# A transformer stack on one Trainium2 core: masks added by VectorE, paired heads in the fourth attention, and output projections with tokens on partitions

## The chip, the core and the metric

The kernel is one program on one core of a Trainium2 chip. Its engines run side by side: TensorE (PE, with its weight loads shown as PEld), VectorE (DVE), ScalarE (ACT), GpSimd (POOL) and SyncE (SP), which here issues DMAs. They meet through semaphores. SBUF and PSUM have 128 partitions; PSUM has eight banks of 512 fp32 columns. The metric is the device time of one execution in microseconds, lower is better.

## The reference

All tensors are fp32. The input is 512 tokens of width 1024 (and 256 context tokens). The first block has two attention layers, the second an even layer (attention and a gated linear recurrence, HGRN), a convolutional feed-forward network (FFN), an odd layer (attention with a relative bias) and a second FFN:

```python
s_loc = jnp.where(valid, s_loc, NEG_INF)                       # attention A: window of 128, sinks, 256 context keys
p = jax.nn.softmax(jnp.concatenate([s_loc, s_ctx, sink], axis=-1), axis=-1)
s = (einsum(qn_b, kn_all) + einsum(qr_b, kr_all)) * scale      # attention B: latent keys, no mask
s = jnp.where(valid, s, -jnp.inf)                              # attention E: chunks of 64, two before, sinks
s = s + bias.reshape(Hkv, G, CHUNK, band)                      # attention O: bias = rel_table[:, clip(i - j)]
c = conv_b + sum(conv_w[j] * u_pad[:, j:j + S]); y = (gelu(c) * v) @ w_down
h = h + rms_norm(y, nw[1])                                     # behind each mixer and each FFN (nw[3])
y = rms_norm(h, nw[2])                                         # ahead of the next one
```

## The kernel before

**Layout.** Activations are kept with features on partitions: `XC[:, k, token]` for the eight groups k of 128 features. Every product is fp32 precision made of three fp32r matmuls: high by high, low by high, high by low (L365 to L367, 512 columns each). Operands are split once: ACT rounds to the high part (`HH`, `WH`) and DVE or POOL subtract to get the low part (`HL`, `WL`). Weights come in panels of 512 KB that SP loads into three slots (`raww`, L1380); ACT writes `WH` (L317) and POOL `WL` (L1481), also three slots each. `lin_bank` takes seven PSUM banks in turn; `claim` makes PE wait until a bank's last reader is done.

**The attentions.** A has 32 jobs (16 heads, four query tiles of 128 rows, and two context tiles, a pair of heads at a time), B 16 heads, E 8 and O 16, with four query tiles each. `finish_att` writes the order of steps down. At step t PE makes the scores of tile t in one of two pairs of banks (`att_scores`, L543), transposes the probabilities of tile t-2 (L615) and multiplies by V, 64 output rows of a head at a time (L651). DVE takes the row maximum (L553; with sinks L556, then L557 on one column), ACT the exponent and its sum (L568) into `PB`, and DVE or ACT copy the transposes out of PSUM into `PT` (L633, L635). Masks of A and E are a bf16 matmul of a mask by the identity into the scores' bank (`maskb`, `identb`). In O the bias is two more matmuls, `flip` by `o_bh` and `flip` by `o_bl`, whose two parts POOL makes per head from a strip `o_band` (L1452, L1454); each O head has its q parts stacked in the 128 rows of `o_q2` and its k parts doubled in `o_kh`, `o_kl` (L1316 to L1320 on ACT, L1329 and L1333 on DVE, 64 rows each). The reciprocals of a pair's sums are turned and spread over 64 rows each by matmuls of 64 output rows (L594: 16 per pair of four tiles, 8 per context pair).

**Out projections and norms.** `e_o`, `o_o` and the down projections give features on partitions: weights are stationary, 512 tokens move (`out_lin`, `ffn_pe`). Down is made in three parts, of 8, 7 and 7 groups of the 22, that DVE adds up. The norm behind each of them (stages s01, s03, s11, s13) needs a sum over partitions: ACT squares (L396), POOL adds (L379), PE sums with ones (L387), ACT takes the root (L406, L409), DVE the reciprocal (L507), and PE spreads it over partitions (L516). Then per k DVE scales (L2419) and adds (L2424), ACT makes `HH` (L467) and a square for the next norm (L471), DVE makes `HL` (L486), and PE starts the next product. L448 sums those squares, four k at a time.

**The end.** The last down part (stage s13) is turned back to tokens by `turn_y` (L1829, four transposes for each of the eight groups), DVE multiplies by the weights (L2591), and behind the norm's sum adds per token tile into `OUTB` (L2362); SP stores four tiles (L1388).

**Panels.** `ahead` bounds how far ACT's part of the splitting goes; SP issues a panel's load when the slot's last product (`last_use`) is done, all in program order.

## Time and profile before

| | us |
|---|---|
| three runs | 2198.93, 2199.13, 2200.2 (median 2199.13) |
| the profiled execution | 2198.79 |
| its span in the trace, first to last instruction | 2196.9 |
| PE, DVE, ACT, POOL busy in it | 2061.3, 1037.0, 890.1, 756.8 |

The profiled execution is 0.3 us under the median, and 1.9 us of it lie outside the span. Times in the trace count from the first instruction. The stages lie at: projections of A from 65 us, attention A 221 to 414, B's projections to 580, attention B 580 to 799, even projections and HGRN 852 to 1016, attention E to 1066, `e_o` to 1114, FFN 0 to 1491, odd projections to 1642, attention O 1642 to 1752, `o_o` to 1797, FFN 1 to 2183. The granted TensorE clock is 1.00 at 2.4 GHz and 0.5 at 1.2 GHz; its mean over the span is 0.977.

### The profile page before, as it was taken

The numbers are of one execution on the slowest core, as the hardware profiler recorded it, in microseconds if no ns is written. First come the engines' busy times: TensorE is split into PE (matmuls) and PEld (weight loads), VectorE is DVE, ScalarE is ACT, GpSimd is POOL, SyncE is SP. The second block draws the span as 40 slices with busy tenths as digits, with TensorE's granted clock in tenths as the row PEclk, the third lists the DMA queues.
The fourth block names the chain that finished last, engine by engine and source line by source line (L and its number), as shares of the span: only waits on it lengthen the run. The fifth ranks groups of instructions, "written<-read, shape, count | busy, mean of one in ns | idle before, by whom it ended". The sixth has DMA issues, their size and how long they took to land.

```text
span 2196.9 us, 29349 instructions
## 1 busy us (share of the span) xinstructions
PE 2061.3 (94%) x11188; PEld 1620.2 (74%) x11188; DVE 1037.0 (47%) x1715; ACT 890.1 (41%) x1644; POOL 756.8 (34%) x446
## 2 busy tenths in 40 slices
PE   5999999999999999998889999998998899999998
PEld 3888655688666667886767888886876677888876
DVE  3420777523366642478337343433137635525253
ACT  4322666423466644545343222224137633222222
POOL 1322122343000144430334444453445543444443
PEclk9999999999999999998999999999999999999998
DMA  7221333132100012320223333332331132333331
GB/s 287 63 63 58 98 105 97 49 109 65 29 1 1 1 39 76 97 69 20 58 77 88 98 100 89 101 92 77 97 91 38 36 87 67 106 96 92 100 98 66
DMA packets 252816, 169.13 MB, mean 77 GB/s; under 512 B 5776, under 2 KB 242039, under 8 KB 251527
## 3 DMA queue, kind: packets, MB, share of 16 engines
q1 hardware_dynamic: 249440, 158.55, 24.5%
q0 software_dynamic: 2192, 8.45, 1.2%
q8 instruction: 92, 1.51, 0.3%
q10 hardware_dynamic: 1047, 0.26, 0.1%
q14 instruction: 45, 0.37, 0.0%
HBM read 165.10 MB, written 2.14 MB: 76 GB/s over the span
## 4 chain that ended last, share of the span: by engine, by line
PE 82%; DVE 8%; issue 4%; ACT 3%; POOL 1%; DMA 0%; ACTq 0%; DVEq 0%; POOLq 0%
PE ps L365 21%; PE ps L366 20%; PE ps L367 20%; PE ps L543 6%; PE ps L651 6%; PE ps L615 3%; PE ps L594 1%; DVE MX L556 1%; DVE PT L633 1%; POOL WL L1481 1%; DVE NB L553 1%; PE ps L987 1%; PE ps L1086 1%; ACT PB L568 1%; DVE o_kl L1333 0%
## 5 line engine op out<-in xcount | busy, mean ns | idle before, releaser
L1481 POOL TENSOR_TENSOR WL<-raww,WH 128x1024 fp32r<-128x1024 f32 (+2 forms) x247 | 582.6, 2363 | 864.3 <-ACT WH L317 852.8
L365 PE MATMUL ps<-HH,WH 128*128 128x512 f32 (+1 forms) x1368 | 525.7, 384 | 28.6 <-DVE HL L486 17.1
L366 PE MATMUL ps<-HL,WH 128*128 128x512 f32 (+1 forms) x1368 | 521.1, 381 | 0.0
L367 PE MATMUL ps<-HH,WL 128*128 128x512 f32 (+1 forms) x1368 | 520.1, 380 | 0.0
L317 ACT ACTIVATE WH<-raww 128x1024 fp32r<-128x1024 f32 (+2 forms) x247 | 254.7, 1035 | 334.2 <-PE ps L367 329.3
L365 PEld LDWEIGHTS ps<-HH,WH 128*128 128x128 f32 x1368 | 260.9, 191 | 88.0 <-issue 30.3
L367 PEld LDWEIGHTS ps<-HH,WL 128*128 128x128 f32 x1368 | 260.6, 191 | 49.1
L366 PEld LDWEIGHTS ps<-HL,WH 128*128 128x128 f32 x1368 | 261.1, 191 | 47.0
L568 ACT ACTIVATE PB<-ps,NB 128x256 f32<-128x256 f32 (+5 forms) x256 | 168.0, 657 | 104.8 <-DVE NB L557 53.0
L615 PE MATMUL ps<-ident,PB 128*128 128x128 f32 x952 | 154.3, 278 | 11.6 <-DVE PT L633 7.1
L651 PE MATMUL ps<-PT,ARENA 128*64 128x512 f32 (+3 forms) x688 | 132.8, 492 | 11.1 <-ACT PT L635 7.8
L365 PE MATMUL ps<-f_h,WH 128*128 128x512 f32 x352 | 137.7, 391 | 1.6 <-DVE f_l L2622 1.6
L367 PE MATMUL ps<-f_h,WL 128*128 128x512 f32 x352 | 137.1, 389 | 0.0
L553 DVE TENSOR_REDUCE NB<-ps 128x1 f32<-128x768 f32 (+4 forms) x128 | 92.5, 723 | 94.3 <-PE ps L543 92.8
L366 PE MATMUL ps<-f_l,WH 128*128 128x512 f32 x352 | 137.0, 389 | 0.0
L615 PEld LDWEIGHTS ps<-ident,PB 128*128 128x128 f32 x952 | 108.5, 142 | 21.9 <-DVE PT L633 12.6
L635 ACT ACTIVATE PT<-ps 128x256 f32<-128x256 f32 (+1 forms) x192 | 83.6, 436 | 89.6 <-PE ps L615 87.6
L2435 DVE TENSOR_TENSOR ARENA<-ps,ARENA 128x512 f32<-128x512 f32 x60 | 40.9, 690 | 156.0 <-PE ps L367 131.0
L2609 DVE SCALAR_TENSOR_TENSOR ARENA<-ARENA,COL 128x511 f32<-128x511 f32 x44 | 110.8, 2519 | 1.6
L2197 ACT ACTIVATE ARENA<-ARENA 128x512 f32<-128x512 f32 x44 | 27.8, 633 | 172.9 <-DVE ARENA L2611 172.9
L556 DVE TENSOR_REDUCE MX<-ps 128x1 f32<-128x512 f32 (+3 forms) x128 | 74.1, 579 | 41.9 <-PE ps L543 41.3
L633 DVE COPY PT<-ps 128x384 f32<-128x384 f32 (+2 forms) x192 | 91.3, 476 | 3.2 <-PE ps L615 2.1
(336 smaller groups left out, 3232.9 us busy)
## 6 DMA issues: line engine op xcount, KB each, us to landing
raww<-in_ffn_w_up SPq DMA_DIRECT2D x88, 512.0 KB, 3.9
raww<-in_ada_w SPq DMA_DIRECT2D x32, 512.0 KB, 3.6
raww<-in_ffn_w_down SPq DMA_DIRECT2D x32, 448.0 KB, 3.7
raww<-in_odd_w_in SPq DMA_DIRECT2D x24, 512.0 KB, 3.7
raww<-in_a_w_in SPq DMA_DIRECT2D x20, 512.0 KB, 3.8
raww<-in_even_w_in SPq DMA_DIRECT2D x17, 512.0 KB, 3.8
raww<-in_ffn_w_down SPq DMA_DIRECT2D x16, 512.0 KB, 3.9
ADA<-in_ada_w SPq DMA_DIRECT2D x6, 1024.0 KB, 16.7
```

The source lines that it names most:

```text
L317: nc.scalar.activation(parts_of(k)[0], raw_slot(k), ACT.Copy).then_inc(*split_hi.mark(k))
L365: nc.tensor.matmul(out, lh, rh, start=start and k == ks[0], stop=False)
L366: nc.tensor.matmul(out, lh, rl, start=False, stop=False)
L367: ins = nc.tensor.matmul(out, ll, rh, start=False, stop=stop and k == ks[-1])
L543: ins = nc.tensor.matmul(ps[:, bk, c0 % 512:c0 % 512 + w], lhs, rhs, start=(q == 0), stop=(q == len(ms) - 1), skip_group_check=True)
L553: nc.vector.tensor_reduce(nb, score_span(A, r, i), AX_X, ALU.max, negate=True)\
L568: nc.scalar.activation(PB[:, t % 4, 0:job["tiles"][i]["n"] * P], score_span(A, r, i), ACT.Exp, bias=NB[:, r % 4, i:i + 1], scale=A["scale" ...
L615: ins = nc.tensor.transpose(ps[:, b, q * P:(q + 1) * P], PB[:, t % 4, (first + q) * P:(first + q + 1) * P], ident[:, :])
L633: nc.vector.tensor_copy(dst, src).then_inc(*pt_dve.mark(*key))
L651: ins = nc.tensor.matmul(ps[p0:p0 + HD, 7, a:z], v, PT[at][:, blk, q0_ + a:q0_ + z], start=(q == 0), stop=(q == n - 1), skip_group_check=True)
L1481: nc.gpsimd.tensor_tensor(lo, raw_slot(k), hi.bitcast(F32), ALU.subtract).then_inc(*split_lo.mark(k))
L2609: chain(dve, dve_step, nc.vector.scalar_tensor_tensor(c[:, 1:S], u[:, 0:S - 1], col(cw, 22 + m), c[:, 1:S], ALU.mult, ALU.add))
```

## The change

1. **Masks.** The masks of A and E become an fp32 constant `masks`. DVE adds them while it takes the row extreme (`tensor_tensor_reduce`, new L641): it writes the negated, scaled, masked scores to `PB` and the least of each row to `NB`. ACT's exponent reads `PB` instead of PSUM. The score banks are free again once DVE has read them. The two-step maximum of the sink jobs and the mask matmuls are gone.
2. **Spread.** DVE copies the reciprocals out to 64 columns each (`RB`, L673) in all four attentions; PE makes one whole 128x128 transpose per tile (L682).
3. **Attention O.** Two heads lie in the two halves of 64 rows. `pair_scores` makes the three products of each, alternating between the halves, a bank per head (L599). DVE adds the bias from `o_band` (four strips) like a mask. The splits are of 128 rows for both heads at once (`o_high`, `o_low`); POOL makes no bias parts. `PT` has four buffers in turn.
4. **Bias rows.** SP copies each head's bias strip 128 times inside DRAM (`rows_dram`, 128x640 fp32 = 328 KB per head), one of these 16 copies behind each of 16 panel loads of FFN 0; POOL reads them with a slant (`band_rows`).
5. **Out projections.** `e_o`, `o_o` and down have tokens on partitions (`out_rows`): activations are stationary, 512 weight columns move, four token tiles by two halves of the columns, over cuts of two groups. The norm is then a row sum that ACT's square gives (`out_square`, `out_root`), DVE scales the left and ACT the right half, PE turns the scaled y back (`between`, 32 transposes, L1641 and L1650), and DVE's `post_norm` is one operation per k that reads PSUM. The POOL sums, L387, L516, L2424 of these stages are gone.
6. **Squares.** `late_parts_act` makes the squares of k from 4 behind all eight `HH`, also at stage s00.
7. **The end.** `turn_y` is gone; POOL multiplies the left and DVE the right half by the weights, DVE adds per token tile and half, and SP stores eight halves of 256 KB.

```diff
-            chain(dve, dve_step, nc.vector.tensor_reduce(MX[:, t % 4:t % 4 + 1], score_span(A, r, i), AX_X, ALU.max))
-            nc.vector.tensor_scalar(nb, MX[:, t % 4:t % 4 + 1], -A["scale"],
-                                    NSINK[:, job["sink"]:job["sink"] + 1], ALU.mult, ALU.min)\
+            if t >= 4:
+                q, j = A["seq"][t - 4]
+                dve.wait_ge(*turned[A["name"], q, j, len(A["jobs"][q]["tiles"][j]["lots"]) - 1])
+            dst, src = PB[:, t % 4, 0:job["tiles"][i]["n"] * P], score_span(A, r, i)
+            if len(add.shape) == 3:
+                dst, src = (x.rearrange("p (a b) -> p a b", a=2) for x in (dst, src))
+            least = NSINK[:, job["sink"]:job["sink"] + 1] if job["sink"] is not None else -NEG
+            nc.vector.tensor_tensor_reduce(dst, src, add, -A["scale"], least, ALU.add, ALU.min, nb)\
...
+            nc.scalar.activation(dst, dst if fused else score_span(A, r, i), ACT.Exp, bias=NB[:, r % 4, i:i + 1],
+                                 scale=-1.0 if fused else A["scale"], accum_out=SUM[:, r % 4, i:i + 1])\
...
+            each = RCP[:, a:a + 2, 0:nq].rearrange("p h (i o) -> p i h o", o=1).to_broadcast([P, nq, 2, HD])
+            nc.vector.tensor_copy(RB[:, 0:nq * P].rearrange("p (i h d) -> p i h d", h=2, d=HD), each)\
+                .then_inc(*rcp_made.mark(A["name"], r))
...
-                for h in (r - 1, r):
-                    p0 = HD * (h % 2)
-                    ins = nc.tensor.matmul(ps[p0:p0 + HD, b, i * P:(i + 1) * P],
-                                           RCP[:, h % 4, i:i + 1].to_broadcast([P, HD]), ident[:, :],
-                                           start=True, stop=True)
+                ins = nc.tensor.transpose(ps[:, b, i * P:(i + 1) * P], RB[:, i * P:(i + 1) * P], ident[:, :])
...
-                                if lo < i:
-                                    parts.append((2 * P, P, identb[:, :], maskb[:, 0:P]))
-                                if hi > i + 1:
-                                    parts.append(((nl + 1) * P, P, identb[:, :], maskb[:, P:2 * P]))
+                                if i:
+                                    add = masks[:, 0:(nl + 2) * P]
+                                else:
+                                    add = masks[:, 0:6 * P].rearrange("p (a b) -> p a b", b=3 * P)[:, :, 0:2 * P]
...
+        def pair_scores(pe, A, r, i):
+            w = A["jobs"][r]["tiles"][i]["n"] * P
+            for h in (r, r + 1):
+                claim(pe, A["at"](h, i) % 4, (max_made, (A["name"], h, i)))
+            A["score_wait"](pe, r, i)
+            for n, (q, k) in enumerate(A["products"](r)):
+                for h in (r, r + 1):
+                    p0 = HD * (h % 2)
+                    ins = nc.tensor.matmul(ps[:, A["at"](h, i) % 4, 0:w], q[p0:p0 + HD, i * P:(i + 1) * P], k[p0:p0 + HD, 0:w],
+                                           start=(n == 0), stop=(n == 2), tile_position=(p0, 0))
+                    if n == 2:
+                        ins.then_inc(*scores_made.mark(A["name"], h, i))
...
-                    parts = [(0, w, o_q2[m % 2][:, i * P:(i + 1) * P], k[m % 2][:, 0:w]) for k in (o_kh, o_kl)]
-                    parts += [(0, w, flip[:, :], b[:, m % 2, 512 - w:512]) for b in (o_bh, o_bl)]
-                    tiles.append(tile(i + 1, parts, [(0, list(range(i + 1)), ("dve", "act")[i % 2])]))
+                    tiles.append(tile(i + 1, None, [(0, list(range(i + 1)), ("dve", "act")[(i + m) % 2])],
+                                      0, o_band[:, m % 4, 512 - w:512]))
...
+        def o_high(act, m, i):
+            if m >= 2:
+                act.wait_ge(*scores_made["O", 2 * m - 3, 3])
+            dst, src, name = (o_qh, o_q, "oqh") if i == 1 else (o_kh, o_k, "okh")
+            nc.scalar.activation(dst[m % 2], src[:, m, :], ACT.Copy).then_inc(*act_out.mark(name, m))
+        def o_low(dve, m, i):
+            hi, lo, src, name = (o_qh, o_ql, o_q, "oqh") if i == 1 else (o_kh, o_kl, o_k, "okh")
+            dve.wait_ge(*act_out[name, m])
+            nc.vector.tensor_tensor(lo[m % 2], src[:, m, :], hi[m % 2].bitcast(F32), ALU.subtract)\
+                .then_inc(*dve_out.mark(name, m))
...
+                m = n - where["up_u", 0, 2]
+                if 0 <= m < 16:
+                    if m == 0:
+                        sp.wait_ge(ext_in, 32)
+                    sp.dma_start(rows_dram[m, :, :], band_dram[m:m + 1, 0:640].to_broadcast([P, 640])).then_inc(rows_out, 16)
...
+            pool.wait_ge(rows_out, 16 * 16)
+            for m in range(4):
+                pool.dma_start(o_band[:, m, :], band_rows(m)).then_inc(band_in[m], 16)
...
+        def out_rows(pe, stage, name, cuts, h_, ready, reader, fill=None, last=False):
+            for i in range(2):
+                for t in range(NT):
+                    claim(pe, lin_bank(stage + (i, t)), *reader(i, t))
...
+                    for t in range(NT):
+                        b = values[("bank", stage + (i, t))]
+                        hs = h_(t * P, P)
+                        for k in range(kn):
+                            if i == 0 and t == 0:
+                                pe.wait_ge(*ready(k0 + k))
+                            ins = split_product(ps[:, b, :], lambda k: hs(k0 + k), lambda k: (wh[:, k, :], wl[:, k, :]), [k],
+                                                c == 0 and k == 0, c == len(cuts) - 1 and k == kn - 1)
...
+        def between(pe, st):
+            for k in range(4):
+                claim(pe, lin_bank(("yp", st, k)), (x_made, (st, k)))
+            for t in range(NT):
+                pe.wait_ge(*dve_out["yn", st, t])
+                for k in range(4):
+                    ins = nc.tensor.transpose(bank(("yp", st, k))[:, t * P:(t + 1) * P],
+                                              y_of[st][:, t, k * P:(k + 1) * P], ident[:, :])
+                    if t == 3:
+                        ins.then_inc(*x_turned.mark(st, k))
+            for k in range(4, 8):
+                claim(pe, lin_bank(("yp", st, k)), (x_made, (st, k)))
+                for t in range(NT):
+                    if k == 4:
+                        pe.wait_ge(*act_out["yn", st, t])
+                    ins = nc.tensor.transpose(bank(("yp", st, k))[:, t * P:(t + 1) * P],
+                                              y_of[st][:, t, k * P:(k + 1) * P], ident[:, :])
+                ins.then_inc(*x_turned.mark(st, k))
...
+            nc.scalar.activation(TMP[:, 2 + t % 2, :], src, ACT.Square, scale=1.0 / 32,
+                                 accum_out=STAT[:, 3, 4 * i + t:4 * i + t + 1]).then_inc(*act_out.mark("ysq", st, i, t))
...
+            nc.scalar.activation(y_of[st][:, t, S:D], src, ACT.Copy, scale=STAT[:, 1, t:t + 1])\
...
+            nc.vector.tensor_scalar(y_of[st][:, t, 0:S], y_of[st][:, t, 0:S], STAT[:, 1, t:t + 1], None, ALU.mult)\
...
-                    nc.vector.scalar_tensor_tensor(y_of[st][:, k, :], y_of[st][:, k, :], col("norm_w_2", 8 * w + k),
-                                                   bank(("rinv", st, 0)), ALU.mult, ALU.mult)\
-                        .then_inc(*dve_out.mark("ynormed", st, k))
-                if 1 <= k < 9:
-                    dve.wait_ge(*dve_out["ynormed", st, k - 1])
-                    nc.vector.tensor_tensor(XC[:, k - 1, 0:S], XC[:, k - 1, 0:S], y_of[st][:, k - 1, :], ALU.add)\
-                        .then_inc(*x_made.mark(st, k - 1))
+                    dve.wait_ge(*x_turned[st, k])
+                    nc.vector.scalar_tensor_tensor(XC[:, k, 0:S], bank(("yp", st, k)), col("norm_w_2", 8 * w + k),
+                                                   XC[:, k, 0:S], ALU.mult, ALU.add).then_inc(*x_made.mark(st, k))
...
+                if k < 4 or k >= 8:
+                    q = k if k < 4 else k - 4
+                    nc.scalar.activation(TMP[:, q % 4, :], XC[:, q, 0:S], ACT.Square).then_inc(*squared.mark(st, q))
...
-        def turn_y(pe, m):
...
+            nc.vector.tensor_tensor(YT[:, t, S:D], y_of[st][:, t, S:D], GROW[:, S:D], ALU.mult)\
+                .then_inc(*dve_out.mark("yg", t))
+            out_recip(dve, st, t)
+            dve.wait_ge(*diag_made[st, t])
+            dve.wait_ge(*dve_out["yg", t])
+            for i in range(2):
+                at = t * D + S * i
+                nc.vector.scalar_tensor_tensor(OUTB[:, at:at + S], YT[:, t, S * i:S * (i + 1)], STAT[:, 1, t:t + 1],
+                                               OUTB[:, at:at + S], ALU.mult, ALU.add).then_inc(*dve_out.mark("out", t, i))
...
+                nc.gpsimd.tensor_tensor(YT[:, t, 0:S], y_of["s13"][:, t, 0:S], GROW[:, 0:S], ALU.mult)\
```

PE in attention O, about the step that makes the scores of 384 columns; `o_kh`, `o_kl` are key parts, `o_bh`, `o_bl` bias parts. Before:

```order
L543 MATMUL ps<-o_kh,o_q 128x384 [waits exp_made]
L543 MATMUL ps<-o_kl,o_q 128x384
L543 MATMUL ps<-o_bh,flip 128x384
L543 MATMUL ps<-o_bl,flip 128x384
L615 MATMUL ps<-ident,PB 128x128 [waits pt_act,exp_made]
L651 MATMUL ps<-PT,ARENA 64x512 [waits pt_dve,pt_act,dve_out]
L651 MATMUL ps<-PT,ARENA 64x512
L594 MATMUL ps<-ident,RCP 64x128 [waits rcp_made,pt_dve]
L594 MATMUL ps<-ident,RCP 64x128 x7
L543 MATMUL ps<-o_kh,o_q 128x512 [waits exp_made]
L543 MATMUL ps<-o_kl,o_q 128x512
```

Now:

```order
L682 MATMUL ps<-ident,RB 128x128 [waits rcp_made,pt_act]
L682 MATMUL ps<-ident,RB 128x128 x3
L701 MATMUL ps<-ident,PB 128x128 [waits pt_dve,exp_made]
L737 MATMUL ps<-o_pt,ARENA 64x384
L737 MATMUL ps<-PT,ARENA 64x384
L599 MATMUL ps<-o_kh,o_qh 128x384 [waits max_made]
L599 MATMUL ps<-o_kh,o_qh 128x384
L599 MATMUL ps<-o_kh,o_ql 128x384 x2
L599 MATMUL ps<-o_kl,o_qh 128x384 x2
L701 MATMUL ps<-ident,PB 128x128 [waits pt_dve,exp_made]
L701 MATMUL ps<-ident,PB 128x128
```

Four matmuls over 128 rows per tile have become three over 64 rows for each of two heads, issued in turn; the spread has half the rows; scores come for two tiles at once, and the transposes and V products of two tiles follow.

DVE in attention O, over about half a pair of heads. Before:

```order
L1329 TENSOR_TENSOR o_q<-ARENA,o_q 64x512 [waits act_out]
L1333 TENSOR_TENSOR o_kl<-ARENA,o_kh 64x512
L553 TENSOR_REDUCE NB<-ps 128x1 [waits scores_made]
L633 COPY PT<-ps 128x128 [waits pv_made,turned]
L1298 TENSOR_TENSOR OT<-ps,BC 128x512 [waits bc_made,pv_made]
L1333 TENSOR_TENSOR o_kl<-ARENA,o_kh 64x512
L553 TENSOR_REDUCE NB<-ps 128x1 [waits scores_made] x2
L633 COPY PT<-ps 128x3x128 [waits pv_made,turned]
L553 TENSOR_REDUCE NB<-ps 128x1 [waits scores_made]
L584 RECIPROCAL RCP<-SUM 128x8 [waits exp_made]
```

Now:

```order
L641 ISA NB 128x1
L719 COPY o_pt<-ps 128x3x128 [waits pv_made,turned]
L1390 TENSOR_TENSOR OT<-ps,BC 128x512 [waits bc_made,pool_out,pv_made]
L641 ISA PB,NB<-ps,ARENA 128x512 [waits turned,scores_made]
L641 ISA NB 128x1
L641 ISA PB,NB<-ps,ARENA 128x128 [waits turned,pool_out,scores_made]
L641 ISA NB 128x1
L641 ISA PB,NB<-ps,ARENA 128x128 [waits turned,pool_out,scores_made]
L641 ISA NB 128x1
L719 COPY PT<-ps 128x4x128 [waits pv_made,turned]
L669 RECIPROCAL RCP<-SUM 128x8 [waits exp_made]
L673 COPY RB<-RCP 128x512 [waits spread_made,dve_step]
```

The 64-row subtractions (six per pair) have become two of 128 rows; each reduction is an ISA row with `PB` as a second output and an ISA row of one column behind it; `RB` is new.

PE from the last matmuls of `o_o` to the first product of FFN 1. Before:

```order
L366 MATMUL ps<-o_ol,WH 128x512
L367 MATMUL ps<-o_oh,WL 128x512
L387 MATMUL ps<-oned,ACC 128x1 [waits summed,o_made]
L387 MATMUL ps<-oned,ACC 128x1 x3
L387 MATMUL ps<-oned,SQ 128x1 [waits squared]
L387 MATMUL ps<-oned,SQ 128x1 x3
L516 MATMUL ps<-ident,STAT 128x128 [waits dve_out,diag_made]
L516 MATMUL ps<-ident,STAT 128x128 x3
L365 MATMUL ps<-HH,WH 128x512 [waits dve_out,split_lo,h_made]
L366 MATMUL ps<-HL,WH 128x512
```

Now:

```order
L1641 MATMUL ps<-ident,ARENA 128x128 [waits dve_out]
L1641 MATMUL ps<-ident,ARENA 128x128 x3
L1650 MATMUL ps<-ident,ARENA 128x128 [waits act_out] x5
L1650 MATMUL ps<-ident,ARENA 128x128 x3
L1650 MATMUL ps<-ident,ARENA 128x128 [waits act_out]
L1650 MATMUL ps<-ident,ARENA 128x128 x3
L1650 MATMUL ps<-ident,ARENA 128x128 [waits x_made]
L1650 MATMUL ps<-ident,ARENA 128x128 x3
L369 MATMUL ps<-HH,WH 128x512 [waits x_made,split_lo,h_made]
L370 MATMUL ps<-HL,WH 128x512
L371 MATMUL ps<-HH,WL 128x512
```

The column sums and the spread are gone from between the products; transposes of `ARENA` (the scaled y) stand there, of which the first 16 wait for DVE and the rest for ACT.

## Rows read from the trace of the kernel before

**Rows 1.** Page, part 4: the chain that ended last, shares of the span by engine.

```profile
PE 82%; DVE 8%; issue 4%; ACT 3%; POOL 1%; DMA 0%; ACTq 0%; DVEq 0%; POOLq 0%
```

**Rows 2.** Busy us of each engine by stretch: A, E, FFN 0, O; clock, DMA share last.

```profile
core 0: us, PE busy (x) PEld busy (x) DVE busy (x) ACT busy (x) POOL busy (x), PEclk, DMA share, GB/s
...
221.00:414.00 193.00, 181.93 (x1462) 113.58 (x1463) 150.97 (x375) 127.29 (x340) 38.29 (x43) 1.00 0.30 88
...
1016.00:1066.00 50.00, 37.54 (x278) 27.41 (x277) 35.59 (x106) 30.22 (x100) 1.25 (x1) 0.81 0.00 1
...
1178.00:1445.00 267.00, 267.00 (x1180) 221.16 (x1179) 120.63 (x122) 73.83 (x87) 118.00 (x52) 1.00 0.35 99
...
1642.00:1752.00 110.00, 95.03 (x634) 66.61 (x633) 79.72 (x152) 82.82 (x208) 53.78 (x69) 0.98 0.11 30
```

**Rows 3.** PE's timeline inside attention A: start us, us, operation.

```profile
252.10 0.28 PE L543 MATMUL ps<-maskb,identb 128*128 128x128 bf16 x2
252.22 0.60 PE L615 MATMUL ps<-ident,PB 128*128 128x128 f32 x4
```

**Rows 4.** Groups of attention A, shapes apart: busy us, mean ns, idle before.

```profile
L557 DVE TENSOR_SCALAR NB<-MX,NSINK 128x1 f32<-128x1 f32 x96 | 20.6, 214 | 3.4
...
L568 ACT ACTIVATION_READ_ACCUMULATOR PB<-ps,NB 128x1 f32 x96 | 18.7, 195 | 0.0
```

**Rows 5.** Chain of one pair of heads in attention O and the next pair's first row.

```profile
1666.71 1.08 PE ps L651 x4
1667.79 0.87 PE ps L594 x16
1668.66 1.12 PE ps L543 x4
...
1680.68 1.08 PE ps L651 x4
```

**Rows 6.** Waits of attention O: us in total, times, longest.

```profile
PEld ps L543 <- ACT PB L568: 18.3, 24, 1.4
...
PE ps L543 <- DVE o_kl L1333: 7.3, 8, 1.2
```

**Rows 7.** Groups of attention O, shapes apart, as in rows 4.

```profile
L1333 DVE TENSOR_TENSOR o_kl<-ARENA,o_kh 64x512 fp32r<-64x512 f32 x29 | 20.2, 698 | 0.4
...
L1329 DVE TENSOR_TENSOR o_q<-ARENA,o_q 64x512 fp32r<-64x512 f32 x14 | 13.4, 959 | 1.2
...
L568 ACT ACTIVATE PB<-ps,NB 128x512 f32<-128x512 f32 x16 | 11.0, 688 | 8.9 <-DVE NB L553 8.1
...
L1316 ACT ACTIVATE o_q<-ARENA 64x512 fp32r<-64x512 f32 x14 | 8.7, 624 | 0.2
```

**Rows 8.** Chain row of the HGRN: 32 matmuls on quarters of the rows, 128 columns.

```profile
943.79 1.10 PE ps L1793 x32
```

**Rows 9.** Timeline from the last `e_o` product through the first two FFN blocks.

```profile
1113.98 0.95 PE L387 MATMUL ps<-oned,ACC 128*128 128x1 f32 x8
...
1118.17 1.41 DVE L2419 SCALAR_TENSOR_TENSOR ARENA<-ARENA,COL,ps 128x512 f32<-128x512 f32 x2 [1.02 <-PE ps L516]
...
1122.25 0.76 PE L365 MATMUL ps<-HH,WH 128*128 128x512 f32 x1 [4.12 <-DVE HL L486]
...
1138.02 1.06 PE L448 MATMUL ps<-TMP,ones 128*32 128x512 f32 x8
```

**Rows 10.** Page, part 5: a DVE operation of two sources, one in PSUM.

```profile
L2435 DVE TENSOR_TENSOR ARENA<-ps,ARENA 128x512 f32<-128x512 f32 x60 | 40.9, 690 | 156.0 <-PE ps L367 131.0
```

**Rows 11.** Timeline of the end: last products' transposes, final additions, stores.

```profile
2182.57 0.60 PE L1829 MATMUL ps<-ident,ARENA 128*128 128x128 f32 x4
...
2188.61 4.87 DVE L2362 SCALAR_TENSOR_TENSOR OUTB<-YT,STAT,OUTB 128x1024 f32<-128x1024 f32 x4
2189.92 3.92 SPq L1388 DMA_DIRECT2D out<-OUTB  x4
```

**Rows 12.** Page, part 6: panel loads, KB each, us from issue to landing.

```profile
raww<-in_ffn_w_up SPq DMA_DIRECT2D x88, 512.0 KB, 3.9
```

514 lines of the change are left out of this document (269 added, 245 removed).

## The prediction, made before the changed kernel was run

> **What bounds the kernel now.** I read the chain of waits first. PE carries 82% of it and DVE 8% [rows 1], so a microsecond taken from PE's line is worth nearly one, except where PE waits. The table by stretches says where that is [rows 2]. In the FFN stretch PE is busy 267.0 of 267 us with about 1180 matmuls; the change keeps every product there (the same 3 matmuls per operand pair, only the stationary and moving sides swapped), so I expect nothing from it. In attention A PE is busy 182 of 193 us: still the bound. In E it is 37.5 of 50 us, at a granted clock of 0.81, so between the full and the half level; in O 95 of 110 us at 0.98. There the loop PE, DVE, ACT, PE is the bound together with PE's work. The rest of PE's idle time lies behind each out projection (the norm that must be finished before the next product) and at the end. I work against the profiled execution of 2198.8 us, 0.3 under the median.
>
> **Masks in A and E.** PE loses 96 mask matmuls in A. In the timeline two of them and the next row start within 0.12 us [rows 3], so 0.06 us each, 5.8 us. On DVE the added source is free as far as rows show: a 128x512 operation with one source in PSUM and one in SBUF takes 690 ns [rows 10], which is what a plain 512-column reduction takes in this kernel too. The L557 step goes, 96 x 214 ns = 20.6 us; each reduction gets a second instruction that reads its accumulator, for which the nearest row is ACT's, 195 ns [rows 4], 18.7 us. DVE comes out even. With PE at 94% of the stage I take the 5.8 us whole.
>
> **Spread, all attentions.** Before a pair's spread, 16 half-wide records take 0.87 to 1.07 us [rows 5]. Four whole 128-column transposes run at the rate of the product behind them: L543 x4 in 1.12 us are four matmuls of 512 columns with a slow first one [rows 5], so 128 columns take about 0.06 (at most 0.07) and four 0.23 us. That is 0.65 us per pair of four tiles and 0.33 per context pair. A has 8 of each: 7.8. B has 8 pairs, 5.2 at most; DVE has there 8 more copies of 128x512 (about 0.5 each) between its maxima, so I take 4. A in sum: 5.8 + 7.8 = 13.6, taken as **-14** (4 if the DVE copies and the longer DVE step delay scores, 20 if L557 was holding PE). B: **-4** (2 to 5).
>
> **E.** 30 mask matmuls at a reduced clock give some 3.5 us, four spreads 2.6, and the score banks come free when DVE has read them, no longer when ACT has made the exponents. PE idles 12.5 us in this stretch, so up to 10 could go; I take **-7** (0 to 10), near the sum of the two priced items.
>
> **Attention O.** A pair takes 1680.68 - 1666.71 = 13.97 us [rows 5], eight pairs 110 us.
> - PE: 95.03/7.87 pairs is 12.1 busy us per pair, 11.8 by start times. The four score matmuls per tile are 4.6 us of it (80 blocks of 128 columns at 0.0575, a quarter of the 0.23 that a 512-column matmul takes: 267.0 us for about 1180 in FFN 0 [rows 2]). Now three products over half the rows, 60 blocks; if the two halves run side by side, 1.7 us, if not, 3.4. That they can is suggested by the HGRN's row: 32 matmuls of 128 columns on quarters of the rows take 1.10 us [rows 8], 0.034 each against 0.0575. The spread saves 0.65. Against it, PE changes more often between whole-array and half-array work: I charge 6 changes at 0.28 us, 1.7 (the odd start-up of L651 and L594 blocks, 1.08 for 4 matmuls of 512 columns where 0.92 is the rate). PE: 11.8 - 2.9 - 0.65 + 1.7 = 9.9.
> - DVE: 79.7/7.87 = 10.1 per pair. Gone: four subtractions of 698 and two of 959 ns [rows 7], 4.7. New: two of 128x512 at 0.69 [rows 10], 1.4; eight accumulator reads at up to 0.2, 1.6; the RB copy 0.5. DVE: 8.9.
> - ACT: 82.8/7.87 = 10.5, six 64-row copies at 0.62 [rows 7] become two: 8.1.
> - Waits: PE loses now 18.3 us to the exponent and 7.3 to the low part of k [rows 6], 3.2 per pair. The second goes (splits are made a pair ahead); of the first, the exponents of 0.69 us [rows 7] remain in the loop, but scores are now two tiles ahead.
> I take PE's 9.9 plus half of what it idles now (2.2): 11.0 per pair, 8 x 2.97 = **-24**. Bounds: 9.2 (all three engines near their busy time), -38, and 13.0, -8.
>
> The Trainium skill, TensorEngine Tiling (Array Packing), Key Properties, says that tiles of different rows load and multiply in parallel, and that changing the tiling mode drains TensorE. By the first the scores would cost the 1.7 us that I use; by the second each switch costs more than a start-up, and at 0.5 us for six switches O would give -14 and not -24. Rows 8 bear out the first; no row shows a drain apart from the start-ups.
>
> **Norms behind e_o, down 0 and o_o.** From the last product to the first of the next stage 8.27 us pass at s01 (1113.98 to 1122.25), 4.1 of it idle at the end, and 24.0 to L448 at 1138.02 [rows 9], for 48 matmuls at 0.23 = 10.9 us; the pattern stands three times in all, with 8.1 us at s03 and 8.5 at s11. Behind it, DVE has three steps per k: scaling (1.41 for two [rows 9]), adding at 0.69 [rows 10] and the low part at about the same. Now, after the last product of the last token tile: ACT square 0.6 and its sum 0.2, root 0.26, reciprocal 0.18, DVE scale 0.4, four transposes 0.3, three STT ahead of the first low part (DVE's order) and that part, 3.0, hops 0.5: 5.4, up to 6.3; I take 5.9, 2.4 earlier. Then DVE needs 1.5 per k instead of 1.9, so 2 to 3 us more would come, of which PE can take about 2, since its products need 10.9 and the first rows after the pause are at the half level (0.76 us for one at 1122.25). I take 4.5 at s01 and s11 and 2.8 at s03 (its wait and its stretch to L448 are shorter, 23.0 us): **-12** (7 to 19). The squares behind all HH give 1 us at s00: **-1**.
>
> **The end.** Seven blocks of four `turn_y` transposes stand between products, 0.6 us each by the row; at 0.06 per 128 columns and a start-up they hold PE for 0.35: 2.1 for the six before the last product. Behind the last product 14.3 us pass (2182.57 to 2196.9): adding, sum over partitions, root, then 4.87 of DVE from 2188.61 [rows 11]. Now the row sum comes from ACT, and DVE has per token tile an add, a product by the weights, a reciprocal and two STT, 3.7 us of which three tiles overlap with the products of later tiles (2.7 us apart). The last tile ends about 6 us behind its product, plus the store of about 3 to 4: 10.2, 4 less. An extra turn_x and closed banks cost 1. **-5** (2 to 7).
>
> **The sum:** -14 - 4 - 7 - 1 - 24 - 12 - 5 = -67, 2198.8 - 67 = 2131.8, over the median's 0.3: 2132. All low ends together are -23 (2176), all high ends -100 (2099).
>
> **DRAM copies.** Between 16 panel loads of FFN 0 SP issues a copy of 328 KB. A panel lasts 5.5 us (24 products), loads 512 KB in 3.9 us to landing [rows 12] and holds the DMA engines for 0.35 of the time [rows 2], 1.9 us. 328 KB by that rate is 1.2 us, doubled for writing DRAM too 2.4: hidden in the 3.6 us free. I cost it at nothing; the cover is gone when a copy takes over 3.6 us.
>
> **Rivals.**
> - *Halves of the rows do not overlap, or switches cost.* Scores 3.4 instead of 1.7, or switches at 0.5: O gives about -12. 2144. For it: no row of two K=64 matmuls alternating. Against: rows 8. Chance 0.12.
> - *The loop stays.* DVE now holds the fused reduction, 0.69 + 0.2, for two heads in a row before the second exponent can start, so that O keeps 13.0. 2148. For it: 18.3 us of exponent waits today [rows 6]. Chance 0.15.
> - *The clock falls in O.* PE gets less busy there; in E, at 75% busy, the clock was 0.81 against 0.98 in O at 86% [rows 2]. At the half level PE's 9.9 becomes about 16 per pair, 128 us: O +18 instead of -24. 2174. Chance 0.10.
> - *The fused reduction runs at half speed.* 0.69 becomes 1.38 at 512 columns; A's DVE then needs some 190 us of 193 and A gains nothing but +15, E +2, O -6: 2188. Against: rows 10, the same two sources at full speed. Chance 0.06.
> - *Slower than before: the copies starve FFN 0.* They sit in SP's queue and on the DMA engines ahead of weight panels. Each costs t - 3.6 us beyond its cover; 16 x (t - 3.6) is over 67 when t is over 7.8 us, that is below 42 GB/s. At 8.5 us: 2210. Against: a load of 512 KB lands in 3.9 us, 131 GB/s. It would decide because nothing else in FFN 0 is idle. Chance 0.05.
> - *The change does not do what it says*: the boundaries keep their 8 us since PE must make all 32 transposes first and the last wait for ACT and for a bank; then -5 instead of -12 there, 2139, within my range. I count it in the forecast's 0.52, which covers 2106 to 2146.
>
> **How the numbers follow.** Forecast 0.52, centre 2132. The range of 2106 to 2168 takes it, the halves and the loop, 0.79, and the mild forms of the clock case. Above it lie clock, half speed and copies. A measurement tells 0.2%, 4.4 us, from no change: slower by more only with the copies (or two bad cases at once), 0.05; within it 0.02; faster 0.93.
>
> **What would show it.** O's period per pair in the chain: 11.0 (right), 13 (loop), 16 at clock 0.5 (clock); inside it, six L599 of 512 columns from first to next operation 0.8 us (side by side) or 1.4. ISA rows of DVE at 0.69 for 512 columns. First product behind the last of `e_o` at 5.9 us. FFN 0's middle 267 us long: longer by more than 5 would mean the copies. DVE's idle time ahead of L641 in A stays on "PE". I am wrong altogether if FFN 0 or FFN 1 loses PE time, on which no term rests.

## The result, and the profile after

| | us |
|---|---|
| before, four runs | median 2199.62 (2198.93 to 2200.20) |
| changed kernel, four runs | median 2132.89 (2130.91 to 2134.41) |
| ratio | 0.9696, 95% interval 0.9679 to 0.9713 |
| spans of the two traces | 2196.9 and 2129.0 |

The prediction was 2132.0, in a range of 2106 to 2168. The total says little about whether its terms were right, so I cut both traces at the same matmuls: the first score product of each attention, the first and last product of each out projection, the first and last of each down projection. `e_o` and `o_o` themselves, 43.4 us each in both traces, are left out; the rest of the span is here:

| stretch | before | after | moved | predicted |
|---|---|---|---|---|
| start to the first score of A | 220.4 | 220.0 | -0.5 | 0 |
| A: first score to `a_o` | 197.2 | 183.4 | -13.8 | -14 |
| `a_o` and B's projections | 173.9 | 176.7 | +2.7 | 0 |
| B: first score to `b_o` | 216.0 | 212.4 | -3.6 | -4 |
| `b_o`, s00, even projections, HGRN | 204.6 | 203.4 | -1.2 | -1 |
| E: first score to `e_o` | 58.3 | 54.5 | -3.8 | -7 |
| last of `e_o` to first of down 0 (s01) | 116.4 | 110.9 | -5.5 | -4.5 |
| down 0 | 260.9 | 260.9 | 0.0 | 0 |
| last of down 0 to first score of O (s03) | 146.5 | 142.3 | -4.2 | -2.8 |
| O: first score to `o_o` | 116.0 | 91.8 | -24.2 | -24 |
| last of `o_o` to first of down 1 (s11) | 116.2 | 110.9 | -5.3 | -4.5 |
| down 1, then to the end | 283.8 | 275.2 | -8.6 | -5 |

The moves add up to -67.9 us, the difference of the two spans; the medians differ by 66.7, since the profiled execution of the changed kernel is 2.0 us under its median.

The busy totals of the page (us, share of the span, instructions):

```profile
PE 2009.5 (94%) x10600; PEld 1569.0 (74%) x10600; DVE 997.8 (47%) x1774; ACT 882.3 (41%) x1668; POOL 698.8 (33%) x394
```

PE is busy 51.8 us less than before, DVE 39, ACT 8. The stretches of A, E and O, against rows 2 (busy us of PE, PEld, DVE, ACT, POOL; clock; DMA share; GB/s):

```profile
219.97:403.37 183.40, 171.31 (x1249) 106.79 (x1248) 143.03 (x392) 129.55 (x342) 40.02 (x44) 1.00 0.32 93
...
995.78:1050.30 54.52, 40.65 (x249) 30.08 (x249) 36.47 (x118) 32.62 (x102) 5.23 (x3) 0.72 0.03 10
...
1607.79:1699.59 91.80, 78.46 (x513) 43.56 (x513) 62.07 (x197) 62.08 (x184) 27.48 (x41) 0.94 0.15 41
```

E's mean clock is 0.72, where the same stretch of before had 0.80; O's is 0.94 where it had 0.98. A's groups of the fused reduction and its read, and of the copy for the spread, against rows 4:

```profile
L641 DVE CUSTOM_DVE_ANT_0 PB<-ps,masks,NSINK 128x640 f32<-128x640 f32 x30 | 26.5, 884 | 16.2 <-PE ps L618 16.2
...
L641 DVE DVE_READ_ACCUMULATOR2_ANT NB<- 128x1 f32 x92 | 7.6, 82 | 0.0
...
L673 DVE COPY RB<-RCP 128x512 f32<-128x512 f32 x8 | 3.4, 426 | 0.3
```

The reduction with its added source takes 884 ns for 640 columns. The read that I had priced at 195 ns from ScalarE's row takes 82. In O, where the least value starts from a constant and not from the column `NSINK`, the same reduction of 512 columns takes what the plain one of before took:

```profile
L641 DVE CUSTOM_DVE_ANT_0 PB<-ps,ARENA 128x512 f32<-128x512 f32 x16 | 10.9, 684 | 0.8 <-PE ps L599 0.8
```

```profile
L553 DVE TENSOR_REDUCE NB<-ps 128x1 f32<-128x512 f32 x16 | 11.0, 690 | 5.4 <-PE ps L543 5.2
```

(after, then before). PE's timeline over one pair of O, against rows 5 (start, us, operation, idle time before and what ended it):

```profile
1640.53 0.66 PE L682 MATMUL ps<-ident,RB 128*128 128x128 f32 x4
1641.02 0.27 PE L701 MATMUL ps<-ident,PB 128*128 128x128 f32 x1
...
1644.43 0.50 PE L599 MATMUL ps<-o_kh,o_qh 64*128 64x512 f32 x2
1644.77 0.39 PE L599 MATMUL ps<-o_kh,o_ql 64*128 64x512 f32 x2
1645.00 0.40 PE L599 MATMUL ps<-o_kl,o_qh 64*128 64x512 f32 x2
1645.32 0.87 PE L701 MATMUL ps<-ident,PB 128*128 128x128 f32 x6
...
1647.03 0.66 PE L701 MATMUL ps<-ident,PB 128*128 128x128 f32 x4 [0.35 <-ACT PB L653]
1648.70 0.66 PE L701 MATMUL ps<-ident,PB 128*128 128x128 f32 x4 [1.01 <-ACT PB L653]
...
1651.24 0.66 PE L682 MATMUL ps<-ident,RB 128*128 128x128 f32 x4
```

A pair takes 1651.24 - 1640.53 = 10.71 us, at a clock of 1.00, where it took 13.97 [rows 5]. Six products of 512 columns start in pairs and are over in 0.89 us. The spread's four transposes take 0.49 to the next row, not 0.23. Twice PE waits for an exponent, 1.36 us in all. Behind `e_o`, against rows 9:

```profile
1093.95 1.07 PE L1641 MATMUL ps<-ident,ARENA 128*128 128x128 f32 x8
...
1097.34 2.07 DVE L2549 SCALAR_TENSOR_TENSOR XC<-ps,COL,XC 128x512 f32<-128x512 f32 x3 [0.42 <-PE ps L1641]
1097.47 1.91 PE L1650 MATMUL ps<-ident,ARENA 128*128 128x128 f32 x16
...
1100.21 0.47 PE L369 MATMUL ps<-HH,WH 128*128 128x512 f32 x1 [0.84 <-DVE HL L490]
```

The last product starts at 1093.72; the next stage's first is at 1100.21, 6.3 us behind its end (8.27 before), and the first row is already back to 0.47 us where it was 0.76 [rows 9]. At the end, against rows 11:

```profile
2123.11 0.68 DVE L2763 TENSOR_TENSOR ARENA<-ps,ARENA 128x512 f32<-128x512 f32 x1
...
2125.16 1.42 DVE L565 SCALAR_TENSOR_TENSOR OUTB<-YT,STAT,OUTB 128x512 f32<-128x512 f32 x2
```

The last product starts at 2119.78 and 9.2 us later all is stored (14.6 before).

### The profile page after: what moved, and what is told of

It reads as the page before. It is cut to its first block, busy times and chain, and to the rows that moved or that the text cites. A ratio compares the mean times of both kernels' runs of the same rounds, so it can differ in the third digit from the quotient of the medians.

```text
span 2129.0 us, 28194 instructions
## 1 busy us (share of the span) xinstructions
PE 2009.5 (94%) x10600; PEld 1569.0 (74%) x10600; DVE 997.8 (47%) x1774; ACT 882.3 (41%) x1668; POOL 698.8 (33%) x394
## 4 chain that ended last, share of the span: by engine, by line
PE 43%; issue 4%; ACT 2%; DVE 2%; POOL 2%; POOLq 0%; DVEq 0%; ACTq 0%
PE ps L369 13%; PE ps L371 13%; PE ps L370 13%; PE ps L737 1%; POOL WL L1563 1%; PE ps L701 1%; PE ps L599 1%; ACT PB L653 0%; ACT TMP L514 0%; PE ps L682 0%; DVE PB L641 0%; PE ps L618 0%; DVE XC L2549 0%; PE ps L448 0%; POOL YT L1551 0%
## 5 line engine op out<-in xcount | busy, mean ns | idle before, releaser
L1563 POOL TENSOR_TENSOR WL<-raww,WH 128x1024 fp32r<-128x1024 f32 (+1 forms) x247 | 583.2, 2366 | 910.1 <-ACT WH L321 901.1
L321 ACT ACTIVATE WH<-raww 128x1024 fp32r<-128x1024 f32 (+1 forms) x247 | 254.7, 1036 | 412.1 <-PE ps L371 408.8
L701 PE MATMUL ps<-ident,PB 128*128 128x128 f32 x952 | 157.5, 283 | 24.5 <-ACT PB L653 16.0
L653 ACT ACTIVATE PB<-PB,NB 128x512 f32<-128x512 f32 (+3 forms) x192 | 116.5, 607 | 72.7 <-DVE NB L641 69.8
L701 PEld LDWEIGHTS ps<-ident,PB 128*128 128x128 f32 x952 | 109.5, 142 | 50.2 <-ACT PB L653 26.9
L369 PE MATMUL ps<-WH,f_h 128*128 128x512 f32 x352 | 137.3, 390 | 1.1 <-DVE ARENA L2763 1.1
L371 PE MATMUL ps<-WH,f_l 128*128 128x512 f32 x352 | 137.0, 389 | 0.0
L370 PE MATMUL ps<-WL,f_h 128*128 128x512 f32 x352 | 136.9, 389 | 0.0
L721 ACT ACTIVATE PT<-ps 128x256 f32<-128x256 f32 (+2 forms) x168 | 70.7, 421 | 79.6 <-PE ps L701 78.0
L631 DVE TENSOR_REDUCE NB<-ps 128x1 f32<-128x768 f32 x64 | 61.1, 955 | 63.7 <-PE ps L618 63.1
L618 PE MATMUL ps<-b_kk,b_qh 96*128 96x512 f32 (+1 forms) x256 | 79.6, 363 | 8.7 <-DVE b_ql L1252 6.8
L719 DVE COPY PT<-ps 128x384 f32<-128x384 f32 (+3 forms) x168 | 82.8, 493 | 8.1 <-PE ps L701 8.0
```

What stands on the lines that cost most here:

```text
L321: nc.scalar.activation(parts_of(k)[0], raw_slot(k), ACT.Copy).then_inc(*split_hi.mark(k))
L369: nc.tensor.matmul(out, lh, rh, start=start and k == ks[0], stop=False)
L370: nc.tensor.matmul(out, lh, rl, start=False, stop=False)
L371: ins = nc.tensor.matmul(out, ll, rh, start=False, stop=stop and k == ks[-1])
L618: ins = nc.tensor.matmul(ps[:, bk, c0 % 512:c0 % 512 + w], lhs, rhs, start=(q == 0), stop=(q == len(ms) - 1), skip_group_check=True)
L653: nc.scalar.activation(dst, dst if fused else score_span(A, r, i), ACT.Exp, bias=NB[:, r % 4, i:i + 1], scale=-1.0 if fused else A["scale" ...
```

## Experiments

All are edits of the changed kernel, timed in three rounds (five where said) beside the kernel before. Their stretches are cut as in the table. An unaltered stretch repeats within 0.3 us from kernel to kernel as long as the clock's dips fall alike; where they don't, it moves by 1 to 3 us (`a_o` and B's projections were 174.0 in one kernel and 176.9 in another with the same work). Two stretches scatter most: E took 54.0 to 56.7 us in nine kernels whose E is the same, at clocks of 0.67 to 0.72, and O 91.8 to 94.5 where the edit doesn't touch it. What an edit does in E can't be read from moves of that size alone. So I read an edit from its own stretch, and its total only to 2 or 3 us.

### Are the halves of the rows side by side, and why

The first edit takes the alternation away, the second also the freedom to overlap.

```diff
-            for n, (q, k) in enumerate(A["products"](r)):
-                for h in (r, r + 1):
+            for h in (r, r + 1):
+                for n, (q, k) in enumerate(A["products"](r)):
```

> The changed kernel, with the scores of attention O made head by head (three products of the upper half of the rows, then three of the lower) instead of alternating. Theory (the halves run side by side only because their matmuls alternate): six matmuls of 512 columns take 1.4 us from first to next operation instead of 0.9, PE has 1.7 us more per pair, and since O's pair of 10.7 us is nearly PE's own work, O gets 8 to 14 us longer: 2141 to 2147. Rival (alternating buys nothing, either because the array overlaps any two halves in flight or because O is bound by its loop): within 2 us of the changed kernel, 2131 to 2135.

Measured: 2132.86 us (2130.48 to 2135.16), O 91.9 us, a pair as long as before the edit. The rival was right. For a tile of 256 columns the program's order is now (names of k and q parts; both heads use the same names):

```text
L599 MATMUL ps<-o_kh,o_qh 128x256
L599 MATMUL ps<-o_kh,o_ql 128x256
L599 MATMUL ps<-o_kl,o_qh 128x256
L599 MATMUL ps<-o_kh,o_qh 128x256
L599 MATMUL ps<-o_kh,o_ql 128x256
L599 MATMUL ps<-o_kl,o_qh 128x256
```

and the loop is the same for 512 columns, yet the trace of this kernel shows pairs there:

```profile
1644.87 0.51 PE L599 MATMUL ps<-o_kh,o_qh 64*128 64x512 f32 x2
...
1645.21 0.40 PE L599 MATMUL ps<-o_kh,o_ql 64*128 64x512 f32 x2
...
1645.44 0.40 PE L599 MATMUL ps<-o_kl,o_qh 64*128 64x512 f32 x2
```

x2 at 1644.87 are the first products of both heads: the second head's started (10 ns behind the first's) while two of the first head's, ahead of it in the program, had not begun. The halves of the rows take their matmuls independently.

```diff
+                    if n == 0 and h == r + 1:
+                        pe.wait_ge(*scores_made[A["name"], r, i])
```

(on top of the head-by-head order)

> The changed kernel, with the scores of O head by head, and TensorE waiting for the first head's three products before it starts the second's, so that the two halves of the rows can't work at once. Theory (side by side is what PE lives on in O): six matmuls of 512 columns take 1.5 to 1.7 us instead of 0.9, PE has 2.5 us more per pair, O +12 to +20: 2145 to 2153. Rival (the loop over the exponents bounds O, and the first head's scores come as early as now): +6 or less, under 2139.

Measured: 2166.82 us (2165.49 to 2168.63), O 126.2 us, +34.4. PE's timeline of one tile of 512 columns:

```profile
1648.75 0.49 PE L601 MATMUL ps<-o_kh,o_qh 64*128 64x512 f32 x1
1649.09 0.39 PE L601 MATMUL ps<-o_kh,o_ql 64*128 64x512 f32 x1
1649.32 0.39 PE L601 MATMUL ps<-o_kl,o_qh 64*128 64x512 f32 x1
1649.77 0.50 PE L601 MATMUL ps<-o_kh,o_qh 64*128 64x512 f32 x1
...
1650.66 0.87 PE L703 MATMUL ps<-ident,PB 128*128 128x128 f32 x6
```

O of this kernel as a stretch, columns as above:

```profile
1609.00:1735.24 126.24, 117.38 (x513) 65.30 (x513) 64.53 (x197) 64.17 (x184) 27.43 (x41) 0.80 0.11 30
```

Two heads one behind the other take 1650.66 - 1648.75 = 1.91 us instead of 0.89. The theory's mechanism holds. Its 12 to 20 us were too few; the clock, which it left out, fell too, to a mean of 0.80 over O, with PE shown busy 117 of 126 us. That is the prediction's clock rival, got by another cause. How the 34 us divide between the serial products and work at 1.2 GHz was not measured apart.

### What pairing is worth beside the added bias

```diff
-                    tiles.append(tile(i + 1, None, [(0, list(range(i + 1)), ("dve", "act")[(i + m) % 2])],
+                    parts = [(0, w, o_q2[m % 2][:, i * P:(i + 1) * P], k[m % 2][:, 0:w]) for k in (o_kh, o_kl)]
+                    tiles.append(tile(i + 1, parts, [(0, list(range(i + 1)), ("dve", "act")[i % 2])],
...
-                            "prep_act": o_prep_act, "prep_dve": o_prep_dve, "paired": True, "products": o_products,
-                            "pt": lambda r: ((4, 2, 5, 6)[r % 4], 0), "pt_free": lambda r: (r - 4) | 1,
+                            "prep_act": o_prep_act, "prep_dve": o_prep_dve,
```

with `o_prep_act` and `o_prep_dve` as before the change (L1309 to L1336).

> The changed kernel, with attention O one head at a time: the two parts of q stacked over the 128 rows as before, two products per tile, six 64-row splits per pair, the old order of steps and three PT buffers; the bias still added by VectorE, the spread still new. Theory (pairing is worth its two halves of the splits: VectorE about 3.3 us and ScalarE 2.5 us per pair more, PE only 0.6): O's pair goes from 10.7 to 12 to 12.7 us, +10 to +16, 2143 to 2149. Rival (nearly all of O's gain came from dropping the two bias matmuls per tile; pairing only rearranges): +4 us or less, under 2137.

Measured: 2153.87 us (2148.35 to 2156.28), O 112.8 us, +21.0, more than the theory's 10 to 16. Without the pairing, 3.2 of O's 24.2 us are left for the dropped bias matmuls and the new spread together. The stretch of O, then the largest wait of PE's products, between 1620 and 1710 us (us in all, times, longest):

```profile
1612.20:1725.02 112.82, 90.22 (x448) 55.24 (x449) 85.12 (x228) 86.33 (x215) 26.22 (x40) 0.82 0.11 29
```

```profile
PE ps L618 <- DVE o_kl L1426: 13.4, 7, 2.1
```

PE is busy 90 of 113 us: it waits 13.4 us (in 90 us of the stretch) for the low part of k, DVE's 64-row subtractions, more than the 7.3 before [rows 6]. The clock is 0.82. The likely reading is that less work for PE was worth little as long as the splits were late, and that part of it came back as a lower clock; the two were not separated. The longest wait points to the subtractions (two per pair instead of six) as what pairing saves; the edit also changes ScalarE's copies and the order of the steps, and these were not tried apart.

### The loop that is left in O

In the changed kernel DVE makes the second head's reduction behind a PT copy and the OT product. Start, us, operation:

```profile
1645.43 0.69 DVE L641 CUSTOM_DVE_ANT_0 PB<-ps,ARENA 128x512 f32<-128x512 f32 x1
...
1646.04 0.55 DVE L719 COPY o_pt<-ps 128x384 f32<-128x384 f32 x1
1646.51 0.68 DVE L1390 TENSOR_TENSOR OT<-ps,BC 128x512 f32<-128x512 f32 x1
1647.11 0.68 DVE L641 CUSTOM_DVE_ANT_0 PB<-ps,ARENA 128x512 f32<-128x512 f32 x1
...
1647.84 0.72 ACT L653 ACTIVATE PB<-PB,NB 128x512 f32<-128x512 f32 x1 [0.48 <-DVE NB L641]
```

The second exponent starts at 1647.84 and PE's wait for it ends at 1648.70.

```diff
-                if r is not None:
-                    att_max(dve, A, r, i)
+                for u in ((t, t + 1) if t % 2 == 0 else ()) if A.get("paired") else (t,):
+                    if att_at(A, u)[0] is not None:
+                        att_max(dve, A, *att_at(A, u))
```

> The changed kernel, with VectorE's two fused reductions of a pair of tiles in O made one after the other, ahead of the PT copy and the OT product that stand between them now. In the changed kernel the second head's reduction of 512 columns starts 1.7 us after the first and PE waits 1.35 us per pair for ScalarE's exponents. Theory (the loop over the second head's exponent bounds O): its exponent starts 1 us earlier, a pair goes from 10.7 to 10.0 us, -4 to -6, 2127 to 2129. Rival (the copies made later hold PE as much as the exponent did): within 1.5 us, 2131.5 to 2134.5.

Measured: 2123.79 us (2122.03 to 2127.33), ratio to before 0.9657 (0.9643 to 0.9671). This beats both kernels. O is 84.7 us, another 7.1 shorter, more than expected; nothing else moved. The timeline of DVE and PE at the 512 columns, then the stretch of O:

```profile
1633.34 0.69 DVE L641 CUSTOM_DVE_ANT_0 PB<-ps,ARENA 128x512 f32<-128x512 f32 x1
...
1633.95 0.69 DVE L641 CUSTOM_DVE_ANT_0 PB<-ps,ARENA 128x512 f32<-128x512 f32 x1
...
1634.94 0.66 PE L701 MATMUL ps<-ident,PB 128*128 128x128 f32 x4 [0.35 <-ACT PB L653]
...
1636.02 0.66 PE L701 MATMUL ps<-ident,PB 128*128 128x128 f32 x4 [0.42 <-ACT PB L653]
```

```profile
1606.98:1691.67 84.69, 75.39 (x512) 42.48 (x513) 59.92 (x197) 61.10 (x184) 24.68 (x40) 0.98 0.13 39
```

The second wait is 0.42 instead of 1.01 us, the period 10.13 (1642.47 - 1632.34) instead of 10.71, eight times 0.58 = 4.6 us. The clock over O went from 0.94 to 0.98, which is where the rest fits: in the changed kernel the pair from 1662.31 on lasts 12.30 us at a clock of 0.87.

The next run added two more orders (five rounds): ScalarE's second exponent ahead of its copy, and the low part one step behind the addition.

```diff
-            for k in range(10):
+            for k in range(9):
...
-                if k >= 2:
-                    late_low(dve, nxt, k - 2, w + 1)
+                if k >= 1:
+                    late_low(dve, nxt, k - 1, w + 1)
```

> The changed kernel with three orders altered: the two fused reductions of a pair of tiles next to each other as in the run with maxima first (that one alone gave 2123.8), ScalarE's second exponent ahead of its PT copy, and behind each norm the low part of k made one step behind the addition instead of two. Theory (what PE waits for in O is still the second exponent, 0.4 us per pair; the first product behind a norm waits for one addition of 0.69 too many): O another 2 to 3 us shorter, the three pauses 0.6 us each, together 2118 to 2121. Rival (the copy made later holds the V products; the low part then waits for ScalarE's high part, and nothing comes of it): within 1.5 us of 2123.8.

Measured: 2126.55 us (2123.59 to 2130.99), not to be told from the run before it. O is 84.9, the three norm stretches are 0.3 us longer. Nothing came of it, as the rival had it. Why O gained nothing is not shown; behind the norms the reason is another than the rival's. PE's first product behind `e_o`:

```profile
1099.12 0.47 PE L369 MATMUL ps<-HH,WH 128*128 128x512 f32 x1 [1.18 <-DVE XC L2553]
```

It waits for an addition (L2553) and not for a low part: its bank is one of those that the turned y fills, and the addition that frees it now stands behind a low part. In the changed kernel the same row waits for the low part (L490), so that two releases lie close together there.

### Masks in A and E

```diff
-                                if i:
-                                    add = masks[:, 0:(nl + 2) * P]
+                                if lo < i:
+                                    parts.append((2 * P, P, identb[:, :], maskb[:, 0:P]))
...
+                chain(dve, dve_step, nc.vector.tensor_reduce(MX[:, t % 4:t % 4 + 1], score_span(A, r, i), AX_X, ALU.max))
```

(the jobs of A and E and the maximum as before the change)

> The changed kernel, with the masks of A and E added by bf16 matmuls, the plain maximum with its second step on one column, and score banks held until the exponent, as before. Theory (the prediction's items: 0.06 us per mask matmul, bank release worth little in A): A +6, E +4, together +8 to +11, so 2141 to 2144. Rival (VectorE's second step and the late release of banks carried the gain in A, mask matmuls little): A alone +10 or more, 2145 or above. Second rival (masks were worth nothing in A because PE then waits for VectorE): A +2 or less, 2133 to 2137.

Measured: 2144.36 us (2143.38 to 2146.80). A 195.2 us, +11.8; E +2.7. The first rival was right in A: the masks bring twice my 5.8 us. E's +2.7, at a clock of 0.79, is as large as its scatter. Two runs divide A's part. The first holds the score banks as long as before:

```diff
-                claim(pe, b, (max_made if job["tiles"][i]["add"] is not None else exp_made, (A["name"], r, i)))
+                claim(pe, b, (exp_made, (A["name"], r, i)))
```

> The changed kernel, with the score banks of A and E claimed until the exponent is made, as before the change, though the exponent no longer reads them; masks still added by VectorE. Undoing the masks as a whole cost 11.8 us in A and 2.7 in E. Theory (the early release of banks is the part of that which the prediction left out): A +4 or more, 2137 to 2141. Rival (the release is worth nothing in A; it was VectorE's second step on one column, 0.21 us, and its share of the latency): A within 1 us, 2132 to 2134.

Measured: 2136.22 us (2135.14 to 2136.53). A +1.2, which is neither the theory's 4 nor nothing, and E +1.3, inside its scatter.

```diff
-            nc.vector.tensor_tensor_reduce(dst, src, add, -A["scale"], least, ALU.add, ALU.min, nb)\
+                mx = MX[:, t % 4:t % 4 + 1]
+                chain(dve, dve_step, nc.vector.tensor_tensor_reduce(dst, src, add, -A["scale"], least, ALU.add, ALU.min, mx))
+                nc.vector.tensor_scalar(nb, mx, 1.0, None, ALU.mult).then_inc(*max_made.mark(A["name"], r, i))
```

> The changed kernel, with a second VectorE instruction on one column (0.21 us, behind a wait for the first) after each fused reduction of A and E, as before the change; its result is a plain copy of the row value. Of the 11.8 us that undoing the masks cost in A, the matmuls are priced at 5.8 and the early release of banks measured at 1.2. Theory (the missing 4.8 us are this second step, which stands between the scores and the exponent on an engine that is busy for 78% of A): A +4 to +6, E +1 to +2, 2138 to 2141. Rival (the step is hidden behind the waits for PE, as it was in the prediction's sum, and the mask matmuls cost twice their spacing): A within 1.5 us, 2132.5 to 2135.

Measured: 2142.07 us (2142.00 to 2142.43). A 191.3 us, +7.9, more than the theory's 4 to 6; E +1.6. The group of the step, then the stretch of A:

```profile
L644 DVE TENSOR_SCALAR NB<-MX 128x1 f32<-128x1 f32 x86 | 13.2, 154 | 3.0
```

```profile
220.06:411.34 191.28, 172.40 (x1249) 106.84 (x1247) 157.73 (x488) 130.91 (x342) 39.55 (x44) 1.00 0.31 89
```

96 such steps of 154 ns (214 before [rows 4]), each with its wait for the one ahead, cost 82 ns of the stage apiece. So of A's 11.8 us, such a step is 7.9 and the early release 1.2, if the parts add up, which was not tried. The 2.7 that are left aren't the price of the 96 matmuls alone, since undoing the masks also brings the plain reduction back, here in that run:

```profile
L633 DVE TENSOR_REDUCE MX<-ps 128x1 f32<-128x640 f32 x28 | 23.1, 824 | 15.1 <-PE ps L620 15.1
```

It is 60 ns shorter than the fused one and has no read of 82 ns behind it. The matmuls may be worth more than 2.7; how much stays open.

### The spread

```diff
-            each = RCP[:, a:a + 2, 0:nq].rearrange("p h (i o) -> p i h o", o=1).to_broadcast([P, nq, 2, HD])
-            nc.vector.tensor_copy(RB[:, 0:nq * P].rearrange("p (i h d) -> p i h d", h=2, d=HD), each)\
...
+                for h in (r - 1, r):
+                    p0 = HD * (h % 2)
+                    ins = nc.tensor.matmul(ps[p0:p0 + HD, b, i * P:(i + 1) * P],
```

> The changed kernel, with the reciprocals spread as before in all four attentions (no RB copy, matmuls of 64 output rows). Theory (the prediction's sum: each pair of four tiles saves PE 0.65 us, context pairs 0.33): A +7.8, B +4, E +2.6, O +5, together +15 to +20, so 2148 to 2153. Rival (attention B moved by only about 1 us in the changed kernel, so the RB copy on VectorE, 0.67 to 0.74 us, eats most of what PE saves): +4 to +9 in all, 2137 to 2142, with B within 1.5 us.

Measured: 2145.91 us (2143.36 to 2147.11), between the two. A +2.6, B +3.5, E -0.4, O +6.8. The rival started from a B that had moved by about 1 us; the table above has 3.6, and the spread is nearly all of it. In A a third of what PE saves comes out. DVE is busy there for 143 of 183 us, so its new copy may be the reason, but it was not tried apart, and at 426 ns it is shorter than in B (683 ns), where two thirds come out. In O the gain is 0.85 us per pair, more than the 0.65 of the sum; the clock over O was 0.91 instead of 0.94, so part of it may be the clock's.

### The norms and the clock

```diff
+                if t == 3:
+                    nc.scalar.preload_act_table(ACT.Exp)
+                    nc.scalar.preload_act_table(ACT.Sqrt)
```

> The changed kernel, with two needless activation table loads (2 x 1.28 us) on ScalarE ahead of the last token tile's square behind e_o and behind o_o, so that PE's pause there is as long as before the change. Theory (part of the gain at these norms is the granted clock: before, 10.2 us at half speed followed the pause at s01 and at s11, and none does now): each pause costs 2.6 us and about 2.5 us more for products at 1.2 GHz, +9 to +11 for the two, 2142 to 2144. Rival (the clock plays no part): +5, 2138, and the clock stays at 1.00 behind both.

Measured: 2140.67 us (2140.10 to 2142.71), +7.8, between theory and rival. s01 +4.2, s11 +3.3, for 2.6 us of delay each; O, which the edit doesn't touch, was 2.7 longer. PE's timeline behind `e_o`, then the two stretches from the last out product on:

```profile
1101.40 1.12 PE L1641 MATMUL ps<-ident,ARENA 128*128 128x128 f32 x4 [3.60 <-DVE ARENA L549]
1102.31 3.62 PE L1650 MATMUL ps<-ident,ARENA 128*128 128x128 f32 x16
1105.58 0.78 PE L369 MATMUL ps<-HH,WH 128*128 128x512 f32 x1
```

```profile
1095.44:1112.00 16.56, 12.55 (x62) 10.41 (x64) 11.50 (x21) 14.21 (x24) 0.00 (x0) 0.79 0.17 51
...
1751.51:1768.00 16.49, 12.48 (x67) 9.48 (x65) 11.58 (x21) 14.29 (x24) 0.00 (x0) 0.90 0.10 29
```

The 16 transposes of the right half take 3.62 instead of 1.91 us. The mean clock is 0.79 and 0.90, in the changed kernel 1.00 over both; the same 14 us of before have 0.64. So beyond its 2.6 us the longer pause costs 1.6 us at s01 and 0.7 at s11. Of the 5.5 us that the change brought at s01, the shorter pause gives 2.0 itself; 3.5 lie behind it. There the kernel before ran its first products at half the clock (columns as in rows 2):

```profile
1122.25:1127.70 5.45, 5.45 (x13) 4.29 (x14) 5.45 (x9) 3.41 (x6) 0.00 (x0) 0.50 0.00 0
```

At the full clock 5.45 us of such products would take half, 2.7 us less, an estimate from this row. DVE's shorter step per k is left for the rest; it was not tried apart.

```diff
-            for k in range(12):
-                if k < 8:
...
+            for k in range(8):
+                act.wait_ge(*ready(k))
...
+                if k >= 4:
+                    act.wait_ge(*statted[st, 3])
```

> The changed kernel, with the squares of k from 4 made between the HH parts again (stages s00, s02, s10, s12). Theory (a square of 0.61 us behind each of four HH, and a wait for PE's L448, delay the last low parts): +1 per stage, four stages, +3 to +5, 2136 to 2138. Rival (VectorE's 1.5 us per k sets the pace and hides them): within 1.5 us.

Measured: 2139.00 us (2137.97 to 2140.76). s01 +1.0, s03 +0.9, s11 +1.0, and s00 +0.7 up to its last early product; behind that the same projections took 3.3 us more with two more dips of the clock. So 3.6 us are the squares, inside the theory's 3 to 5. The rest of the 6.1 goes with the clock: E and O, which the edit doesn't touch, were longer too, by 2.2 and 1.2.

### The DRAM copies

```diff
+                    for q in range(1, 4):
+                        sp.dma_start(rows_dram[16 * q + m, :, :], band_dram[m:m + 1, 0:640].to_broadcast([P, 640]))\
```

> The changed kernel, with each of the 16 DRAM copies issued four times (to rows that nothing reads), so 64 copies of 328 KB between the same 16 panel loads of FFN 0. In the changed kernel a copy lands 5.1 us after its issue and the median panel load went from 3.9 to 4.3 us. Theory (the slower rival of the prediction: what a slot's copies need beyond 3.6 us is paid 16 times): four copies need 5 to 10 us of the DMA engines, +20 to +95 us, 2153 to 2228. Rival (three panel slots and copies that share the engines with loads hide even four): +5 us or less, under 2138.

Measured: 2153.10 us (2152.76 to 2155.77), +20.2, the low end of the theory. From `e_o` to down 0 +16.3, down 0 +4.3, nothing elsewhere. The DMA queue of this kernel from 1140 to 1250 us (packets, MB, share of 16 engines), then PE's waits there:

```profile
q1 hardware_dynamic: 19518, 24.93, 86.9%
```

```profile
PE ps L370 <- POOL WL L1568: 16.2, 12, 2.2
```

With four copies the engines of q1 are 87% busy and a panel slot lasts 7 to 8 us instead of 5.5. A copy is 128 packets of 2560 bytes. They take 110 ns on average in the changed kernel's trace and 174 in this one, which makes 0.9 and 1.4 us of the 16 DMA engines per copy, on either side of the 1.2 from which the prediction started. One copy per slot stays under its cover of 3.6 us. The changed kernel issues its 16 between 1092.7 and 1188.4 us, ahead of down 0, and the stretch from `e_o` to down 0 takes 110.9 us, as long as the same work behind `o_o`, which has no copies. Down 0 took 260.89 us in every kernel but this.

## Why the prediction was right, point by point

- **A** (-14, measured -13.8): right in sum, wrong in parts. "DVE comes out even" was the failing step: the accumulator read is 82 ns and not 195, the reduction is 60 ns longer, and the step that went (L557) stood on the path. Such a step was worth 7.9 us, which I had put at 0, though I had named it as what could take A to 20. The masks brought 11.8 and not 5.8; the spread 2.6 and not 7.8. I charged its copy on DVE in B and not in A; whether that is why is open.
- **B** (-4, -3.6; 3.5 come back with the spread undone): right, and nearly all spread. **s00** (-1, -1.2): the squares are worth 0.7 there by their own run, but the stretch around it took 202.3 to 205.2 us with the same work, so its -1.2 shows nothing by itself. The 2.7 us lost between A and B, on which no term rests, are the clock: the mean over B's projections went from 0.95 to 0.92 with the same matmuls, and with the two orders above the stretch took 174.0, as before the change.
- **E** (-7, -3.8): no term of it is shown. Undoing the masks moved it by 2.7, holding the banks by 1.3 and the old spread by -0.4, none more than the 2.7 us by which E scatters with the same work. The run without the masks had a higher clock in E (0.79), so its 2.7 can hardly be lost clock and the masks are likely worth something there; the old spread had 0.81, which may hide what the spread brings. The changed kernel's E had 0.72 where it had been 0.80; how much that cost is open.
- **O** (-24, -24.2; 11.0 per pair, 10.7): right in size, and the halves do run side by side (0.89 us for six of 512 columns, 0.8 forecast). A switch between whole and half rows costs 0.1 to 0.15 us and not the 0.28 that I charged: from the start of the last L599 of 512 columns to the next L701 pass 0.32 us, of which 0.23 are the product, and from the last V product of 128 columns to the first L599 0.20, of which some 0.06 are the product. The Trainium skill, TensorEngine Tiling (Array Packing), Key Properties, has "Mode switching requires drain"; no cost of 0.5 us, as in my rival, shows here. The other property that the Trainium skill lists there, that different tiles work in parallel, is what the two runs on the halves show. In a pair at full clock PE is busy 9.3 us, where I had 9.9, and waits 1.4, where I had 1.1. But PE's own work carries less than I said: without pairing its matmuls take some 0.6 us per pair more (40 blocks of 128 columns at 0.0575 us instead of 60 at half of that), and O gets 21 us longer. DVE's two subtractions instead of six, in the prediction an item of DVE's sum and 7.3 us of waits, are where the waits point.
- **Norms** (-12, -15.0): the first product came 2.0 us earlier, 2.4 forecast. The term that was too small is "of which PE can take about 2": it kept the half-speed rows behind the pause, and they went.
- **End** (-5, -8.6): 5.3 behind the last product instead of 4.1; and the 3.3 ahead of it are more than turn_y's 2.1, against which I had charged 1 us for an extra turn_x and closed banks; no run shows that cost.
- **Rivals.** Halves don't overlap: no. The loop stays: partly, 0.6 us per pair of it, which the run with maxima first removes. The clock falls in O: not here (0.94), but to 0.80 with the halves in turn and 0.82 unpaired. Fused reduction at half speed: no, 0.68 us for 512 columns. Copies starve FFN 0: four per panel do, one doesn't; at 1.4 us each two would still be under the cover, an estimate from that run. The change is all there.

So +2.7 (clock) and +3.2 (E) stand against -3.0 (norms) and -3.6 (end), and inside A two larger errors cancelled. That the centre was hit to 1 us is partly luck.

## What to carry to other kernels

Ask of a short instruction not how long it is but whether it stands between two engines: a step on one column cost 82 ns of the stage each time, though its engine was idle a fifth of the time. When a reduction must serve several streams in turn, issue the reductions together and let the copies follow; that one reordering was worth a third of all that the pairing brought (7.1 of 21.0 us, each with the clock's part in it). Cut two traces at the same matmuls and compare stretch by stretch, with the granted clock beside each, before any total is believed.

## What the runs showed that I had not expected

- Matmuls on one half of the rows (64 of 128) start ahead of earlier ones of the other half: 10 ns behind the first, with two before them in the program.
- DVE's accumulator read is 82 ns, ScalarE's 187 to 195.
- Adding a second source to DVE's reduction cost nothing (684 ns for 690 at 512 columns); with a column as its start value it took 60 ns more than the plain one (884 for 824 at 640).
- The granted clock had a mean of 0.80 over a stretch in which the profile shows PE busy for 93% of the time (halves in turn), and of 0.98 over one with 89% (maxima first). The busy share alone doesn't say which clock a stretch will have.
- Writing 328 KB from DRAM to DRAM in rows of 2560 bytes takes 0.9 us of the 16 DMA engines with one such copy per panel load, and 1.4 us with four.
